# First layer, U phase: 32 more tokens by gathered rows, 352-column products, and a third weighted one-hot row on ScalarE

## The reference

```python
def peer(h, w_pq, sub_keys, u_tab, v_tab):          # T tokens, D = 1024
    q = (h @ w_pq).reshape(B, T, 8, 2, 64)
    s = einsum('bthcd,hckd->bthck', q, sub_keys)     # 128 keys on each of two sides
    top_s, top_i = lax.top_k(s, 16)
    cand = top_s[..., 0, :, None] + top_s[..., 1, None, :]
    best_s, best_j = lax.top_k(cand.reshape(B, T, 8, 256), 16)
    i1 = take_along_axis(top_i[..., 0, :], best_j // 16, -1)
    i2 = take_along_axis(top_i[..., 1, :], best_j % 16, -1)
    expert = i1 * 128 + i2                           # 8 heads x 16 = 128 experts a token
    w = softmax(best_s)
    u, v = u_tab[expert], v_tab[expert]              # rows of two 16384 x 1024 tables
    act = gelu(einsum('cd,ced->ce', h, u), approximate=False)
    return einsum('ce,ced->cd', act * w, v)
```

## Time and profile before

| | |
|---|---|
| median of 3 runs | 3246.27 us (3245.52 to 3247.68) |
| the profiled execution | 3238.48 us |
| its span | 3236.4 us |
| mean granted PE clock | 0.958 |
| busy share of PE, DVE, ACT, POOL | 93%, 76%, 47%, 29% |
| U phase of layer 0 | 394.4 to 1063.3 us |
| V phase of layer 0 | from 1068.0 us |

### The profile page before, as it was taken

One profiled execution on the slowest core, in us unless ns is written; L12 is line 12 of the kernel. 1 busy time (PEld: TensorE's weight loads), 2 busy tenths in 40 slices (PEclk: granted clock), 3 DMA queues, 4 the chain that ended last, 5 costly groups with the idle time before them and its releaser, 6 DMA issues.

```text
span 3236.4 us, 49042 instructions
## 1 busy us (share of the span) xinstructions
PE 3009.5 (93%) x19164; PEld 2657.7 (82%) x19164; DVE 2451.3 (76%) x4976; ACT 1536.5 (47%) x2895; POOL 942.6 (29%) x835
## 2 busy tenths in 40 slices
PE   6998999999999999999979899899999999988898
PEld 4656799989999888888765899888998899755898
DVE  2696588897888688888758678897999866668654
ACT  3455335737557333333444547496555543232543
POOL 0000046565656344344000024454685200000000
PEclk9999999999999999999998999999999999967899
DMA  7384347969789999999527568899999867501444
GB/s 233 97 283 157 127 159 273 341 242 315 271 286 339 370 371 353 381 357 368 174 96 256 182 227 315 278 351 361 380 400 400 325 207 247 158 33 47 155 142 132
DMA packets 352934, 824.41 MB, mean 255 GB/s; under 512 B 20256, under 2 KB 216384, under 8 KB 332608
## 3 DMA queue, kind: packets, MB, share of 16 engines
q1 hardware_dynamic: 257216, 469.79, 41.8%
q0 software_dynamic: 93120, 347.17, 29.3%
q10 hardware_dynamic: 2368, 4.32, 0.4%
HBM read 747.76 MB, written 73.40 MB: 254 GB/s over the span
## 4 chain that ended last, share of the span: by engine, by line
PE 65%; DVE 22%; DMA 6%; ACT 4%; issue 2%; POOL 1%; DVEq 0%; SPq 0%; ACTq 0%; POOLq 0%
PE ps L1021 16%; PE ps L944 16%; PE ps L639 13%; DVE fr L1823 5%; DVE area L1831 4%; DVE area L1823 3%; DMA ring<-in_peer_v 3%; PE ps L1000 3%; PE ps L1109 2%; PE ps L717 2%; PE ps L1101 2%; PE ps L873 2%; DVE plain L2259 1%; ACT fr L1265 1%; PE ps L919 1%
## 5 line engine op out<-in xcount | busy, mean ns | idle before, releaser
L1823 DVE TENSOR_TENSOR fr<-ring,fr 128x1024 fp32r<-128x1024 f32 x641 | 781.7, 1222 | 473.3 <-ACT fr L1265 470.5
L1265 ACT CAST fr<-ring 128x1024 fp32r<-128x1024 f32 x677 | 703.7, 1045 | 566.5 <-PE ps L1021 323.5
L944 PE MATMUL ps<-fr 128*128 128x384 f32 (+1 forms) x4784 | 851.0, 331 | 14.2 <-DVE fr L1823 14.1
L944 PEld LDWEIGHTS ps<-fr 128*128 128x128 f32 x4784 | 789.2, 191 | 19.5 <-DVE fr L1823 17.1
L1021 PE MATMUL ps<-fr 128*128 128x512 f32 x2304 | 523.9, 390 | 4.4 <-DVE fr L1823 4.4
L1021 PEld LDWEIGHTS ps<-fr 128*128 128x128 f32 x2304 | 433.4, 188 | 94.8 <-ACT area L1582 4.7
L639 PE MATMUL ps<-fr 128*128 128x256 f32 (+1 forms) x2928 | 415.3, 304 | 26.2 <-DVE fr L1823 26.2
L639 PEld LDWEIGHTS ps<-fr 128*128 128x128 f32 x2928 | 389.1, 193 | 52.3 <-DVE fr L1823 32.5
L2680 POOL DMA_INDIRECT plain<-in_peer_v,area x192 | 284.9, 1484 | 259.6 <-DVE area L1831 167.0
L1046 PE MATMUL ps<-fr 128*128 128x384 f32 x1024 | 297.6, 362 | 12.9 <-DVE fr L1823 12.4
L2712 POOL DMA_DIRECT2D g_scratch<-area x224 | 127.0, 567 | 581.1 <-ACT area L1582 540.9
(11 more groups left out here) (228 smaller groups left out, 3990.5 us busy)
## 6 DMA issues: line engine op xcount, KB each, us to landing
ring<-in_peer_uT SPq DMA_DIRECT2D x128, 1024.0 KB, 6.2
ring<-in_peer_v SPq DMA_DIRECT2D x128, 1024.0 KB, 10.0
ring<-in_w_mod SPq DMA_DIRECT2D x48, 1024.0 KB, 5.3
w_scratch<-acc POOLq DMA_DIRECT2D x36, 1024.0 KB, 8.4
g_scratch<-area POOLq DMA_DIRECT2D x128, 192.0 KB, 5.2
area<-g_scratch POOLq DMA_DIRECT2D x64, 384.0 KB, 8.8
area<-w_scratch POOLq DMA_DIRECT2D x16, 1536.0 KB, 10.0
ring<-in_w_ada SPq DMA_DIRECT2D x24, 1024.0 KB, 5.1
```

Source lines behind the costliest of these rows:

```text
L944: ins = e.matmul(o[:, 0:width], pairs[m][0], pairs[m][1], start=(m == 0), stop=(l == 0 and m == last), skip_group_check=l == 1)
L1265: e.copy(hi, x).then_inc(act.after(("high", name)), 1)
L1823: return e.tensor_tensor(o, a, b, op).then_inc(dve.after(*labels), 1)
```

## The change

It does five things in layer 0, and one in both layers.

1. `EXTRA = (32, 0)`: 32 more tokens (128 to 159) have their U rows gathered: 160 rows in place of 128, the 32 new ones as rows 16 to 47 (`FIRST_EXTRA`). One gather serves 32 tokens x 4 experts, so h and the index table are laid out four times (`hx2`, `idx2`: eight more TENSOR_SCALARs of 96 and eight of 32 columns, eight more transposes on PE, two more ACT copies, three small DMAs). The rows now come 2 a tile.
2. The U products and gelu are 352 columns wide. G keeps 384 columns; its first 32 are ones, and the weight of an extra token in W is multiplied with its gelu instead (`xt`, `xw`), so the V phase is as before. The extras' eight quads come last (`QUADS`), and DVE makes all four weighted rows of these; blocks 1, 2 and 3 have 24, 32 and 40 quads.
3. In every second group ACT makes the weighted rows of three tokens and DVE of one.
4. `AHEAD_STEPS`: PE does four steps more before it waits for `ww`, and four fewer in the next block's first fill; in layer 1 too, where ACT does the same with three.
5. At the end of the U phase POOL's loads of W and G stand in another order; the gathers of V rows begin one by one.
6. DVE's search buffers are smaller or shared (`SW`, `cand` in `eq`).

```diff
+AHEAD_STEPS = {"pe": (4, 4), "act": (0, 3)}
+def act_tokens(l, quad):
+    if QUADS[l][quad] < EXTRA[l] // 4:
+        return ()
+    return (0, 1, 2) if l == 0 and quad % 2 == 0 else (0, 1)
+EXTRA = (32, 0)
+FIRST_EXTRA = 16
...
-                pairs = M.three(lambda s, k: v[s][:, k, :], lambda s, k: HR[:, s, k, b.first:T], range(8))
+                pairs = M.three(lambda s, k: v[s][:, k, :], lambda s, k: HR[:, s, k, b.first + EXTRA[l]:T], range(8))
...
-                fill(fill_a)
+                fill(fill_a - (early_steps if h4 == 0 else 0))
             fill(2 * fill_b)
             fill(2 * fill_c)
             if 128 * (t + 1) <= b.first:
                 continue
+            early_steps = AHEAD_STEPS["pe"][l]
+            fill(early_steps)
+            if (l, t) == (0, 2):
+                n = EXTRA[l]
+                w.wait_ge(dve, ("urow", l, FIRST_EXTRA + n - 1))
...
             w.wait_ge(dve, ("ww", l, t))
...
-        for j in sorted({0, 1, 2, 3} - set(ACT_TOKENS)):
+        for j in sorted({0, 1, 2, 3} - set(act_tokens(l, quad))):
...
+            n = extra_row(l, k)
+            if n is None:
+                m = main_row(l, k)
+                h, dot = b.hx, b.dot[:, m:m + 1]
+            else:
+                w.wait_ge(act, ("hx2", l, 1))
+                h, dot = b.hx2, b.dot2[:, n:n + 1]
...
-        fill(5)
+        fill(5 + 5 * l)
         w.wait_ge(pe, ("ow", l, D // 4 - 1))
         w.wait_ge(dve, ("oh", l, D // 4 - 1))
         load_g(KEPT[l] // 2 + 0)
-        fill(5)
         for i in range(2):
             w.wait_ge(M.w_stored[i], ("w", l, nst - 2 + i))
         load_w(0)
+        fill(5)
+        load_g(KEPT[l] // 2 + 1)
+        fill(5)
+        load_w(1)
         fill(3)
-        load_g(KEPT[l] // 2 + 1)
-        load_w(1)
-        fill(5)
```

## The result

| | before | changed |
|---|---|---|
| median of 20 runs each | 3241.01 us (3234.34 to 3247.68) | 3250.37 us (3238.92 to 3264.83) |
| ratio, 95% interval | | 1.0028 [1.0019, 1.0038] |
| the profiled execution | 3238.48 us | 3256.93 us |
| its span | 3236.4 us | 3255.1 us |

What follows compares the result with a forecast made beforehand. It took PE to bound layer 0's quads and block 0, DVE the searches of blocks 1 to 3; -4.6 + 1 - 4 + 3 + 0 + 0 - 2.3 = -6.9 us gave a median of 3239.4 us, range 3220 to 3258.

Steps and rivals of the forecast that it cites:

- second rival: Layer 0's quads: the loop of four row buffers sets a slower pace, 5.9 us a tile, +14, 3254 us; chance 0.27.
- Quads, the rows' side and the DMA side: Layer 0's quads: row-buffer loop and DMA load together keep the pace of before, 5.66 us a tile; 0 us.
- a slower pace relieves the DMA engines, and the two meet between 5.5 and 5.9. I take 5.66: Layer 0's quads: loop and landings balance at the pace of before, us a tile; 0 us, bounds -17 and +14.
- if the rows decide: Sign among block 1's quads: five quads take over 17.3 us if the rows set the pace, 17 as forecast.
- Searches and behind `ti`: Layer 0, blocks 1 to 3: searches -4 us from closer score products, stretches behind `ti` +3.
- PE now idles longer in front of `ti`: Layer 0, blocks 1 to 3: longer idling lowers the clock behind `ti`, +1 each, +3; bounds 0 and +6.
- Block 0: Layer 0, block 0's search: 72 steps get shorter by narrower products, -4.6 us; two more ACT copies before, +1.
- Quads, PE's side: Layer 0's quads: narrower products let PE take 3.21 us a quad, -17 us over 88 quads if others keep up.
- From U to V: End of layer 0's U phase: W's load lands sooner but two U rows stand behind it; 0, bounds -3 and +3.
- Layer 1: Layer 1, block 1's search: the first DVE wait for score products ends four steps sooner, -2.3 us.
- The memory ceiling: Layer 0's quads: a rival where the memory's bytes set the pace, 6.28 us a tile, 3249 us; chance 0.03.

Runs made afterwards that it cites:

- no_ahead: The changed kernel with the steps ahead taken out in both layers, ACT's too; ratio to the kernel before 1.0059.
- six_slots: The changed kernel with a fifth row buffer from block 2 and a sixth from block 3, same bytes; ratio to the kernel before 0.9941.
- no_extra_two: The changed kernel without extra tokens (384 columns) and with two weighted rows on ACT, steps ahead and load order kept; ratio to the kernel before 0.9944.
- loads_only: The kernel before with only the new order of POOL's loads and the smaller search buffers; ratio to the kernel before 1.0007.
- columns_only: The changed kernel with 352-column products but the 32 extra tokens not computed, no gathers or dot products for them; ratio to the kernel before 0.9871.
- no_row_dma: The changed kernel without the gathers of the 32 extra rows, DVE working on what lies in the buffers; ratio to the kernel before 0.9999.
- two_tokens: The changed kernel with two tokens' weighted rows on ACT in every group, as before; ratio to the kernel before 1.0031.
- mild_late: The changed kernel with six buffers and 1.85, 1.95, 2.2 rows a tile in blocks 1, 2, 3; ratio to the kernel before 0.9964.
- late_rows: The changed kernel with six buffers and 1.75, 1.85, 2.4 rows a tile in blocks 1, 2, 3; ratio to the kernel before 0.9966.

## Why the prediction was wrong

It gave 3239 us (-6.9) where the change cost 9.4 us; the median, 3250.4, lay in its range, and near the 3254 of its second rival, the rows' loop. It failed in two terms of opposite sign, +25.0 and -13.0 against the forecast, and that the time lay in the range is owed to their cancelling in part.

- **Quads, the rows' side and the DMA side (0; measured +25.0).** The failed step is "a slower pace relieves the DMA engines, and the two meet between 5.5 and 5.9. I take 5.66". The loop was worked out rightly (a landing of 9.5 gives 12.2 us, 6.1 a tile), and 6.0, 6.1 and 6.3 us a tile came. But nothing met: in `no_ahead`, with the same loop, the rows still took 9.0 to 9.6 us to land at 342 to 358 GB/s, far under the 395 at which the earlier trace rows had 11.4. So the landing of 9.5 was right, and the 6.1 that it gives by the forecast's own sum was the answer; it was given up for a relief, to a landing of 8.6 by that sum, that did not come. The 8.4 of the earlier trace rows (8.0 over all 29 rows of that block) belonged to a stretch in which a row was asked for every 3.8 us, not every 3.1. The step took the pace of before as the place of balance, though with two rows a tile the loop has 2 tiles of slack and not 2.67. Its own sign for this came: five quads of block 1 take 17.8 us, over the 17.3 of "if the rows decide". `six_slots` shows the loop as the cause: same bytes, more buffers, 3.30 in place of 3.80.
- **Searches and behind `ti` (-4 and +3, -1 in sum; measured -14.0).** Up to `ti` the three took 68.1, 67.3 and 69.9 us (before 68.9, 72.0 and 70.8): -6.4 for -4, within the bounds, though block 2 gave most of it and not block 3. The failed step is "PE now idles longer in front of `ti`" and the +3 put for it; the stretches behind `ti` took 12.9, 13.3 and 11.2 us (before 14.5, 16.2 and 14.4), -7.7, outside the bounds of 0 and +6, at clocks of 0.87, 1.00 and 1.00, not 0.85 and 0.89. PE waited 2.4, 0.6 and 2.4 us in front of `ti`, where 8 had been forecast for block 2. The sum 5.4 + 4.6 - 2 leaves out the 3.1 us of steps that fill this very wait; without them (`no_ahead`) PE did wait longer in blocks 1 and 3, 5.4 and 6.3 us for 3.3 and 3.4, and the clocks behind `ti` were 0.80 to 0.82. And in block 1 the steps come on top, 366 matmuls before `ti` and not 348, as its own first fill is not shortened. "The four steps ahead do not shorten DVE's chain; they only fill PE's wait" was right, as far as it goes (last score product to `ti`, in `no_extra_two`); it was what a filled wait is worth that was put at nothing. `no_extra_two` against `loads_only` (244.2 and 256.8 us) and the changed kernel against `no_ahead` (242.8 and 256.0) both show it as the work of the steps. The rows and the narrower products, -4 to +3 in the forecast's terms, came out near nothing.
- **Block 0 (-4.6; measured -3.0)**, the same in `columns_only`. (The +1 for two ACT copies lies in the stretch before it, which varied by 10 us, and was not told apart.) A 352-column matmul starts 0.159 us after the last (a chain of 12 takes 1.91 us among the quads; expected 0.161), but the 256 of block 0 took 42.84 us, 0.167 each, in the chain below: they did not run at that pace there. In `six_slots`, `no_row_dma`, `two_tokens` and `mild_late`, with the same work in block 0, they did (41.05 us for 258 in the second line below), and block 0 took 62.8 to 63.2 us, 5.0 to 5.4 less than before. So the term was sized rightly for one of two paces that the chain has, and what chooses between them stays open. The chain of the changed kernel, and a line of that of `six_slots`:

```profile
413.97 5.19 PE ps L988 x30
419.16 1.08 PE ps L1026 x8
420.24 42.84 PE ps L988 x256
```

```profile
421.27 41.05 PE ps L1011 x258
```

- **Quads, PE's side**: right as a mechanism (3.21 a quad; 3.19 in columns_only), and the ceiling was given rightly as one. ACT's casts held nothing up: in `columns_only` DVE waited 11.7 us for them in block 1 (16.0 before), and PE did not wait.
- **From U to V (0, bounds 3; measured +1.9).** The order of the loads did what was said, both ways. The chain after the last quad:

```profile
1057.54 8.78 DMA w_scratch<-acc
...
1066.85 0.57 POOL area L2870
...
1067.72 0.54 POOL area L2773
...
1069.01 11.29 DMA area<-in_peer_u,area
```

The load of W (L2870) goes out when the last store has landed, and the last rows behind it (L2773) now end the phase, where the earlier trace rows had the load of W.
- **Layer 1 (-2.3; measured -1.4)**: right, with the slower quads as a cost that was not seen.
- **The memory ceiling (0.03, at 352 GB/s at a share of 1.0)** rightly had a small chance: it lies at 390 to 395 GB/s, where only the versions with six buffers came to it. The Trainium skill, page "DMA: Bandwidth & Descriptors", section Bandwidth, has about 358 GB/s as the HBM limit of one core, and gives it as each core's part when both cores of an HBM domain stream. The changed kernel's 344 to 356 GB/s look like it, but `six_slots` moved 395 in the same stretch, so the trace does not agree with it as a limit for one core that runs alone.

So the change is a gain of 16 us (steps ahead, layer 0), one of 21 (columns), and a loss of 45 (the 32 tokens' rows; 640.2 to 685.7 us), with 1.4 for the loads. Of the 45, 29 go away with two more buffers (`six_slots`, 656.7); the other 16 are what the rows cost with six, and were not taken apart. Between the end of layer 0's V phase and layer 1's first scores the kernels without extra tokens took 254.5 to 255.9 us, those with them 257.0 to 260.3, the kernel before 258.8; why stays open. Two versions beat both kernels by most: six_slots (0.9941), with all that the change does, and no_extra_two (0.9944), without the extra tokens; their U phases differ by 4.5 us, no more than the 5.0 of block 0 alone, and their times by nothing that was measured. With six buffers the 32 tokens just pay for their rows.

## What to carry to other kernels

When an operation is moved from a busy engine to a gather with few buffers, work out the loop first: buffers over (landing under that load + the consumer's work and its queue + the request), and compare it with the rate wanted; 1.75 rows a tile passed through four buffers nearly at PE's pace, 2 did not, and no balance came to the rescue. When work is moved in front of a wait of PE, count what it does to the clock behind the wait, even where the wait's end does not move: four steps in front of `ti` took 16 us off this phase, half of them in the stretches behind `ti`, 32 gathered tokens with six buffers 4. And test the parts of a bundle alone: here one part carried the gain and another hid it.

## What the runs showed of the hardware

- A DMA share near 1 does not say that the DMA engines are at their limit. Among quads they had a share of 0.96 to 0.98 at 338, 344, 350, 356 and 362 GB/s (in `no_ahead` 0.95 at 342, 0.99 at 358), 0.99 at 372, and 1.01 at 375, 377, 388, 389 and 395. Two more buffers took block 3 from 344 GB/s at 0.97 to 395 at 1.01.
- The time of a gather to landing went up with the load (the middle over all rows of a block): 8.0 us at 338 GB/s and one row every 3.8 us, 9.0 to 9.6 at 342 to 358 GB/s and one every 3.1 to 3.3 (`no_ahead`), 9.4 and 9.2 at 362 and 377 GB/s and one every 3.3 and 3.1, 10.7 at 389 and one every 2.7 (`late_rows`). Bytes and the number of gathers under way rise together here; which of them counts was not tested.
- The granted clock behind a wait of PE: 0.80 after 3.3 us, 0.85 after 5.4, 0.89 after 3.4; 1.00 after 2.2 (`no_extra_two`), 0.87 and 1.00 after 2.4 (the changed kernel's blocks 1 and 3). The same 70 matmuls took 14.6 us at 0.80 and 11.9 at 1.00.
- The start of a matmul after the last one: 0.227 us for 512 columns, 0.174 for 384, 0.159 for 352. That is 0.42 ns a column between the first two and 0.47 between the last two. The chain of block 0 at 352 columns ran at 0.167 in some kernels and at 0.159 in others, each throughout.
